# Transposing the dense hidden activations outside TensorE: VectorE 32x32 blocks and two DMA passes through DRAM

## The reference, cut to what matters

```python
h = rms_norm(x, ffn_norm_g[l])                       # (256, 1024)
u = silu(h @ w_gate[l]) * (h @ w_up[l])              # (256, 2816)
x = x + u @ w_down[l]                                # (256, 1024)
```

## Time and profile before

| | |
|---|---|
| median of the runs | 2260.6 us |
| the profiled execution: time, span | 2262.25 us, 2261.0 us |
| TensorE busy in the span | 2241.1 us (99%) |
| VectorE, ScalarE, GpSimd busy | 1733.3, 1370.5, 83.6 us |
| granted TensorE clock, share of 2.4 GHz | 0.998 |
| traffic of DMA | 586.05 MB, mean 259 GB/s |

### The profile page before, as it was taken

One profiled execution on the slowest core, in us unless ns is written; L12 is line 12 of the kernel. 1 busy time (PEld: TensorE's weight loads), 2 busy tenths in 40 slices (PEclk: granted clock), 3 DMA queues, 4 the chain that ended last, 5 costly groups with the idle time before them and its releaser, 6 DMA issues.

```text
span 2261.0 us, 30455 instructions
## 1 busy us (share of the span) xinstructions
PE 2241.1 (99%) x12336; PEld 1926.5 (85%) x12336; DVE 1733.3 (77%) x2226; ACT 1370.5 (61%) x1794; POOL 83.6 (4%) x106
## 2 busy tenths in 40 slices
PE   9999999999999999999999999999999999999997
PEld 6998888898888999888899888888888888888886
DVE  6976556877554578655678898989998899989898
ACT  5654444655443454444454587777777777777775
POOL 2200001300000000000100000000000000000001
PEclk9999999999999999999999999999999999999999
DMA  7455453545544435555434599999999999999996
GB/s 260 161 185 193 176 200 145 178 169 214 188 182 149 179 131 210 189 199 189 151 107 170 225 360 383 378 357 376 379 385 362 364 376 389 366 362 374 386 373 245
DMA packets 95891, 586.05 MB, mean 259 GB/s; under 512 B 21968, under 2 KB 23296, under 8 KB 26624
## 3 DMA queue, kind: packets, MB, share of 16 engines
q1 hardware_dynamic: 80496, 568.75, 66.9%
q10 hardware_dynamic: 13664, 9.52, 1.5%
q0 software_dynamic: 1584, 5.77, 0.6%
HBM read 579.27 MB, written 4.73 MB: 258 GB/s over the span
## 4 chain that ended last, share of the span: by engine, by line
PE 95%; DVE 2%; issue 1%; ACT 1%; DMA 1%; POOL 0%; ACTq 0%; DVEq 0%
PE bank L480 28%; PE bank L482 28%; PE bank L481 28%; PE bank L477 9%; PE bank L710 2%; PE bank L756 1%; DVE wl L1617 1%; PE bank L510 1%; DMA raw<-in_ws 1%; POOL SM L2469 0%; PE bank L804 0%; ACT wh L1163 0%; DVE BIAS L1963 0%; DVE X L2330 0%; DVE X L2376 0%
## 5 line engine op out<-in xcount | busy, mean ns | idle before, releaser
L1617 DVE TENSOR_TENSOR wl<-raw,wh 128x1024 fp32r<-128x1024 f32 x698 | 820.1, 1223 | 229.1 <-ACT wh L1163 225.7
L1163 ACT ACTIVATE wh<-raw 128x1024 fp32r<-128x1024 f32 x704 | 704.5, 1054 | 305.5 <-PE bank L482 264.6
L480 PE MATMUL bank<-wh,GH 128*128 128x512 f32 x896 | 352.7, 394 | 0.0
L482 PE MATMUL bank<-wh,GL 128*128 128x512 f32 x896 | 349.3, 390 | 0.0
L481 PE MATMUL bank<-wl,GH 128*128 128x512 f32 x896 | 348.9, 389 | 0.0
L1617 DVE TENSOR_TENSOR wl<-spare,wh 128x1024 fp32r<-128x1024 f32 x264 | 310.0, 1221 | 30.4 <-ACT wh L1163 28.0
L1163 ACT ACTIVATE wh<-spare 128x1024 fp32r<-128x1024 f32 x264 | 264.2, 1054 | 58.9 <-PE bank L482 56.8
L480 PE MATMUL bank<-HH,wh 128*128 128x256 f32 x832 | 239.6, 288 | 0.0
L481 PE MATMUL bank<-HL,wh 128*128 128x256 f32 x832 | 235.3, 283 | 0.0
L482 PE MATMUL bank<-HH,wl 128*128 128x256 f32 x832 | 235.3, 283 | 0.0
L480 PE MATMUL bank<-wh,HH 128*128 128x512 f32 (+1 forms) x600 | 224.9, 375 | 2.5 <-DVE wl L1617 2.3
(11 more groups left out here) (295 smaller groups left out, 3420.7 us busy)
## 6 DMA issues: line engine op xcount, KB each, us to landing
raw<-in_ws SPq DMA_DIRECT2D x352, 1024.0 KB, 6.3
spare<-in_ws SPq DMA_DIRECT2D x132, 1024.0 KB, 7.0
more<-in_ws SPq DMA_DIRECT2D x48, 1024.0 KB, 4.8
once<-in_ws SPq DMA_DIRECT2D x4, 1024.0 KB, 12.0
scratch_parts<-Y POOLq DMA_DIRECT2D x7, 512.0 KB, 8.4
REL<-in_relb ACTq DMA_DIRECT2D x4, 768.0 KB, 12.8
LNB<-in_ln ACTq DMA_DIRECT2D x3, 1024.0 KB, 5.8
LNB<-in_ln ACTq DMA_DIRECT2D x4, 512.0 KB, 4.3
```

What stands on the lines that cost most here:

```text
L480: T.q.matmul(o, l[0], r[0], start=start, stop=False)
L482: return T.q.matmul(o, l[1], r[0], start=False, stop=stop)
L1163: A.q.activation(sets[c % NSET][0][:, half * i:half * i + half], raws[stream.place[n]][:, half * i:half * i + half], ACT.Copy).then_inc(*h ...
L1617: V.q.tensor_tensor(wl[:, half * i:half * i + half], raw[:, half * i:half * i + half], wh[:, half * i:half * i + half].bitcast(f32), ALU.s ...
```

## The change

In the three dense feed forwards (`tiles == 2`) TensorE's transposes, their PSUM groups and ScalarE's and VectorE's reads of these go. Instead:

- VectorE's product of `TT` and `gu` is written in another column order (a, f, r), and right behind it VectorE transposes `TU[t]` in 32x32 blocks into the new `TB[t]` (`v_blocks`). From chunk 1 on it first waits until the previous chunk's `TB` has been written out.
- GpSimd (`g_hidden`) issues all DMAs: for each chunk two that write `TB[t]` to DRAM (128 rows of 2 KB each), a wait until the second has landed, and four that read back 32 partitions each, in pieces of 512 B (256 B for the last chunk), into `TURNED[c % 2]`.
- ScalarE (`a_hidden`) waits for the four and rounds both tiles of the chunk into `FH` in one instruction of 128x1024, and VectorE (`v_hidden`) puts the remainder into `FL`. Chunks 0 to 3 have their place two chunks later, chunks 4 and 5 at steps 1 and 4 of the down product.
- TensorE's down product waits for `hidden_done` where it waited for the emptied `tu` group.

```diff
@@ t_swiglu
-                left += [(c, t, n) for t in range(tiles)]
+                if tiles == 1:
+                    left.append((c, 0, n))
@@ t_feed_forward
-            turn = t_swiglu(s_hidden, HV, lambda k, t: out("h", 2 * l + 1, t, k // 4), F_CHUNKS, 2, l,
-                            first=lambda: t_turn_x(2 * l + 1, 1))
-            t_down(s_down, FV, lambda k, t: out("tu", l, k // 4, t), 22, "dn", l, 2, turn,
+            t_swiglu(s_hidden, HV, lambda k, t: out("h", 2 * l + 1, t, k // 4), F_CHUNKS, 2, l,
+                     first=lambda: t_turn_x(2 * l + 1, 1))
+            t_down(s_down, FV, lambda k, t: hidden_done.at(l, k // 4), 22, "dn", l, 2,
                    tail=lambda: t_turn_x(2 * l + 2, 0))
@@ ScalarE
+        def a_hidden(l, c):
+            src, hi_part, _ = turned_parts(c)
+            A.wait_ge(*blocks_in.at(l, c, 3))
+            A.q.activation(hi_part, src, ACT.Copy, scale=1.0).then_inc(*part.mark("hidden", l, c))
@@ a_down (v_down likewise)
-                if i == 0 and after_first:
-                    after_first()
+                if last_chunks and i in (1, 4):
+                    last_chunks(4 + i // 4)
@@ a_swiglu (v_swiglu likewise, with v_hidden)
                 turn()
+                if tiles == 2 and c >= 2:
+                    a_hidden(i, c - 2)
@@ VectorE
+        def v_hidden(l, c):
+            src, hi_part, lo_part = turned_parts(c)
+            V.wait_ge(*part.at("hidden", l, c))
+            V.q.tensor_tensor(lo_part, src, hi_part.bitcast(f32), ALU.subtract).then_inc(*hidden_done.mark(l, c))
+
+        def v_blocks(l, c, t, n):
+            V.wait_ge(*out("gu", l, c, t))
+            if c:
+                V.wait_ge(*blocks_out.at(l, c - 1, 1))
+            V.q.transpose(TB[t][:, 0:n], TU[t][:, 0:n]).then_inc(*blocked.mark(l, c, t))
@@ GpSimd, called behind g_norm(2 * l + 1)
+        def g_hidden(l):
+            for c, (c0, c1) in enumerate(F_CHUNKS):
+                n = c1 - c0
+                for t in range(2):
+                    G.wait_ge(*blocked.at(l, c, t))
+                    G.q.dma_start(bass.AP(blocks.tensor, 131072 * c + 128 * n * t, [[n, 128], [1, n]]),
+                                  TB[t][:, 0:n]).then_inc(*blocks_out.mark(l, c, t))
+                G.wait_ge(*blocks_out.at(l, c, 1))
+                if c >= 2:
+                    G.wait_ge(*hidden_done.at(l, c - 2))
+                for a in range(4):
+                    G.q.dma_start(TURNED[c % 2][32 * a:32 * a + 32, 0:2 * n].rearrange("p (b n) -> p b n", b=8),
+                                  bass.AP(blocks.tensor, 131072 * c + n // 4 * a, [[n, 32], [32 * n, 8], [1, n // 4]])
+                                  ).then_inc(*blocks_in.mark(l, c, a))
```

## The result

The changed kernel takes 2245.55 us (median of 4 runs, 2245.3 to 2245.83) against 2260.41 (4 runs) before: 14.86 us or 0.66% less. The ratio is 0.9932, with a 95% interval of 0.992 to 0.9945. The forecast was 2245.8 us.

The account below looks back on a forecast made before the run. TensorE, busy for 99% of the span, was taken to bound the kernel. Removed transposes at 4.95 us a layer made 14.8 us over three layers, additions 0: 2260.6 - 14.8 = 2245.8 us, range 2244.0 to 2251.

Parts of the forecast that it names:

- What bounds: Dense feed forward: TensorE busy without a gap, so an instruction taken away shortens the path by its whole cost.
- 0.90 us a packet: TensorE, dense feed forward: cost of eight transposes and the changes between them and products; 4.95 us a layer.
- The room: Dense feed forward: some 6 us left after rounding a weight slot, so TensorE doesn't see VectorE's added transposes.
- The trip: Turned data's way out to DRAM and back in, dense feed forward: taken as 18 us, bounds 12.6 to 38.5.
- the budget: Chunk 4's round trip may take 28.4 us, data landing by E4 + 29.8, before TensorE starves.
- E4 + 18.9: When ScalarE gets to `a_hidden` of chunk 4, behind the rounding of down slot 3, in us.
- E4: End of chunk 4's products in a dense feed forward, the point from which the prediction measures distances.
- E4 + 29.8: Latest landing of chunk 4's data, in us, before TensorE starves for the rounding of down slot 4.
- Rival 1: Round trip late at ScalarE's wait for chunk 4: each us over 28.4 costs TensorE 3 us in all; chance 0.09.
- its worst case: Chunk 4's trip at the worst of each row, 38.5 us: +15.5, 2276 us.
- Rival 2: Chunk 4's trip slightly late (28.4 to 33 us), or chunk 5's: 1 to 4 us lost a layer; chance 0.08.
- Rival 3: Time comes back in a later stage, above all the experts (DMA at 0.95): 2256 to 2260 us; chance 0.03.

Follow-up runs that it names:

- five sets: Changed kernel with chunk 4's four reads from DRAM made five times, each set behind the landing of the one before: 2273.89 us, ratio 1.0055 to the kernel before.
- four sets: Changed kernel with chunk 4's four reads from DRAM made four times, one set after the other: 2259.17 us, ratio 0.9994 to the kernel before.

## Why the prediction was right

- **What bounds.** The windows without a gap were the right ground. Putting the transposes back, and nothing else, gave 2260.46 us, the time of the kernel before.
- **0.90 us a packet.** Predicted 4.95 us a layer from the distance between packets; measured 4.95, 5.00 and 5.01 from mark to mark. Reading the duration (272 ns in the earlier trace rows) would have given 36 us instead of 14.8: the products are pipelined and only distances add up.
- **VectorE.** Predicted 0.69 us for a 128x512 transpose, measured 0.712. The room was said to be 6 us; 4.5 us more were put in without any loss, and more wasn't tried. The changed column order of the product, priced at nothing, costs nothing: 0.679 us instead of 0.680 (medians in the dense layers).
- **The trip.** This is the one term that was mis-sized: I took 18 us, it is about 10. A write of 256 KB lands in 2.9 us and a read of 128 KB in 512 B pieces in 5.0, while my ends came from 512 KB transfers in the experts (8.4 us) and a 768 KB load (12.8 us). I corrected too little for the load of the DMA: the same write of 256 KB lands in 2.9 us in the dense layers and in 6.1 and 7.4 us in the experts with two and four chunks moved, at DMA shares of 0.99 and 1.00. What the size alone is worth wasn't tried. It did no harm, since the budget was 28.4. An estimate by the figure of the Trainium skill (DMA: Bandwidth & Descriptors, section Anatomy of one DMA), 2.0 us + bytes/436e3 us, gives 2.6 and 2.3 us: near the 2.9 of the write here, half of the 5.0 of the read.
- **The budget.** E4 + 18.9 for ScalarE's arrival is in the trace to a tenth. E4 + 29.8 for TensorE's first idle time was tested at E4 + 28.0 (none), 32.6 (2.82 us) and 37.3 (7.51 us) in layer 0, and in the other layers of the same runs: it holds to 0.1 us. A range for the trip that lay under this number was what made the forecast safe, more than the trip's own value.
- **Rival 1** had the right place, and the right price for the idle time itself, but lacked the clock: in the runs of five and four sets the loss was a third and a half more than the idle time, so its worst case was priced too low. **Rival 2** didn't occur: ScalarE's row for chunk 4 names no idle time. The warning of the Trainium skill (VectorE: DVE Perf Modes, section The three transpose paths) about a plain DMA that transposes by strides doesn't bite where blocks of 32x32 are turned first and runs of 512 B are moved: 5.0 us to landing. The form that it warns of was run in no kernel here.
- **Rival 3**, that the experts give the time back, is shown wrong: from ScalarE's first copy to Y to the end of the span it is 851.5 us before and 851.2 after, and the run with fewer transposes there shows that TensorE bounds the stage.

## What to carry to other kernels

Where TensorE has no gap, a transpose on it costs its distance from start to start (0.11 us here, not the 0.27 of its record), and it can be bought off with idle VectorE and DMA time if the result isn't wanted for a few tens of us. Before you do it, work out the latest time at which the data may land from what is *queued behind* the wait on the waiting engine, not from when the data themselves are read: here that was E4 + 29.8, although TensorE first reads chunk 4 at about E4 + 55. And do it only as far as the DMA has room: two expert chunks of seven gained 6.7 us, with four all of that was gone and some 4 us more.

## What the runs showed of the hardware

- After gaps of 2.8, 5.9, 7.5 and 10.7 us TensorE came back at the lower of its two clock levels for some us, products 0.43 us apart instead of 0.23. After the gap of 4.05 us (five sets, layer 1) it came back at the upper level, 0.23 us apart, and fell to the lower one 1 us later, for 3.3 us. After 0.54 and 0.07 us it stayed at the upper level. Over all three layers, mark to mark, 8.8 us of idle time cost 13.6 us, and 22.3 us cost 29.5. Layer 1 lost less (0 and 6.0 us) than layer 2 (9.1 and 13.9) because its data came earlier, by 6.9 and 6.7 us of ScalarE's wait; why its reads were faster is open.
- GpSimd issues a DMA of 256 pieces of 512 B in 0.59 us, no more than one of 128 rows of 4 KB (0.58 in the earlier trace rows); the 4 us an issue that rival 1 allowed for is not seen.
- The same four reads of 128 KB, made one set after the other, took 9.2, 7.9, 6.0 and 4.7 us from start to start in layer 0 of the run of five sets. They ran beside the weight loads, which run out while ScalarE stands; that these are the cause wasn't tried.
